# Attention on one Trainium2 core: three PSUM banks for the turned probabilities, one for the values

## The reference, cut to what matters

```python
# selected blocks (all blocks are selected here: 16 of 16), 4 heads of 64, 1024 tokens, blocks of 128 queries
s = jnp.einsum('bqhd,bqkd->bhqk', q, kg) * ATTN_SCALE - slopes[None, :, None, None] * dist[:, None]
p = _masked_softmax(s, ok[:, None])
return jnp.einsum('bhqk,bqkd->bqhd', p.astype(vg.dtype), vg)
...
# sliding window of 512 keys: the same, with 0 <= dist < 512
...
# forgetting attention: s + (fq - fk), keys up to the query, values of its own for each head
```

## Time and profile before

| | us |
|---|---|
| median of three runs | 1512.06 |
| lowest and highest | 1507.91 and 1513.5 |
| the profiled execution, as timed | 1509.91 |
| its span, first to last instruction | 1508.3 |
| TensorE busy with matmuls, of the span | 1368.0 (91%) |
| VectorE, ScalarE, GpSimd busy | 611.7, 516.6, 368.3 |

### The profile page before, as it was taken

How to read it: one execution, slowest core, us unless ns; L and a number is a source line. 1 busy time by engine, 2 the same in 40 slices (tenths; PEclk the granted TensorE clock), 3 DMA queues, 4 the chain that set the end, 5 groups by cost and what they waited for, 6 DMA issues and landing times. The chain is left out here.

```text
span 1508.3 us, 23664 instructions
## 1 busy us (share of the span) xinstructions
PE 1368.0 (91%) x8917; PEld 1185.3 (79%) x8917; DVE 611.7 (41%) x1593; ACT 516.6 (34%) x962; POOL 368.3 (24%) x463
## 2 busy tenths in 40 slices
PE   5999999999999999978888978979985999999965
PEld 3999999999888989956665657968865888888832
DVE  6222212222423324034667557863563233333317
ACT  5422222222122221126545656530001333434336
POOL 5211150020202000002333214621133322322307
PEclk9999999999999999969999999989995999999978
DMA  7244393162624224872004018762117787888954
GB/s 211 71 156 147 122 245 117 58 180 72 188 58 152 78 69 69 186 213 40 1 2 161 16 40 265 233 213 84 63 35 189 237 286 250 265 280 273 326 220 181
DMA packets 188963, 228.29 MB, mean 151 GB/s; under 512 B 47607, under 2 KB 157303, under 8 KB 187487
## 3 DMA queue, kind: packets, MB, share of 16 engines
q1 hardware_dynamic: 176270, 186.25, 41.1%
q0 software_dynamic: 12592, 40.71, 8.7%
HBM read 167.89 MB, written 60.19 MB: 151 GB/s over the span
## 5 line engine op out<-in xcount | busy, mean ns | idle before, releaser
L1255 PE MATMUL psum<-proj_x_hi,proj_w_hi 128*128 128x362 f32 (+1 forms) x1056 | 357.4, 338 | 3.4 <-DVE proj_w_lo L1380 2.2
L1255 PE MATMUL psum<-proj_x_hi,proj_w_lo 128*128 128x362 f32 (+1 forms) x1056 | 346.9, 329 | 0.0
L1255 PE MATMUL psum<-proj_x_lo,proj_w_hi 128*128 128x362 f32 (+1 forms) x1056 | 346.8, 328 | 0.0
L1255 PEld LDWEIGHTS psum<-proj_x_hi,proj_w_hi 128*128 128x128 f32 x1056 | 199.6, 189 | 10.4 <-POOL proj_x_lo L1461 2.5
L1255 PEld LDWEIGHTS psum<-proj_x_lo,proj_w_hi 128*128 128x128 f32 x1056 | 199.9, 189 | 0.0
L1255 PEld LDWEIGHTS psum<-proj_x_hi,proj_w_lo 128*128 128x128 f32 x1056 | 199.3, 189 | 0.0
L1380 DVE TENSOR_TENSOR proj_w_lo<-proj_w_raw,proj_w_hi 128x1024 fp32r<-128x1024 f32 x44 | 54.4, 1237 | 273.8 <-ACT proj_w_hi L1288 273.7
L1317 ACT ACTIVATE proj_sig<-psum,proj_bias 128x362 f32<-128x362 f32 (+1 forms) x72 | 40.4, 564 | 240.6 <-PE psum L1255 228.0
L2809 PEld LDWEIGHTS psum<-moe_xgt,expert_gate_w 128*128 128x128 f32 x512 | 85.2, 194 | 13.2 <-issue 13.2
L2809 PE MATMUL psum<-moe_xgt,expert_gate_w 128*128 128x192 f32 x512 | 92.1, 334 | 0.7 <-ACT moe_xgt L2854 0.7
L2809 PE MATMUL psum<-moe_xgt,expert_up_w 128*128 128x192 f32 x512 | 88.4, 326 | 0.0
(11 more groups left out here) (479 smaller groups left out, 2406.6 us busy)
## 6 DMA issues: line engine op xcount, KB each, us to landing
proj_w_raw<-in_w_in SPq DMA_DIRECT2D x43, 512.0 KB, 5.1
expert_gate_w<-in_moe_w_gate SPq DMA_DIRECT2D x16, 1024.0 KB, 5.6
expert_up_w<-in_moe_w_up SPq DMA_DIRECT2D x16, 1024.0 KB, 11.1
expert_down_w<-in_moe_w_down SPq DMA_DIRECT2D x16, 1024.0 KB, 8.0
merge_sig<-gate_scratch SPq DMA_DIRECT2D x24, 544.0 KB, 4.1
gate_scratch<-proj_sig SPq DMA_DIRECT2D x48, 181.0 KB, 2.0
feature_scratch<-proj_feat SPq DMA_DIRECT2D x13, 512.0 KB, 3.0
token_scratch<-proj_tok SPq DMA_DIRECT2D x10, 512.0 KB, 5.2
```

Of the source, the lines that this page charges most:

```text
L1255: mm = nc.tensor.matmul(k.ps[u % RING][:, 0:w], b[wt][:, x % 2, kk, :], b[xx][:, kk, a0:a0 + w], start=(kk == 0 and i == 0), stop=(kk == K ...
```

## The change

The groups of turned probabilities go round three banks, 4, 5 and 6, so that a group waits for the copy of the group three before it and no more for that two before it. The values of all units are accumulated in bank 7, so that the values of unit u wait for the output of unit u - 1, and no more for that of unit u - 2. Nothing else is touched: the number of instructions and their order are the same on every engine.

```diff
-    bank_of = {x: 4 + n % 2 for n, x in enumerate(groups)}
+    bank_of = {x: 4 + n % 3 for n, x in enumerate(groups)}
...
                     G = groups_upto(u) + g
-                    if G >= 2:
-                        name, count = copied(*groups[G - 2])
+                    if G >= 3:
+                        name, count = copied(*groups[G - 3])
                         pe.wait_ge(s[name], count)
...
                 pe.wait_ge(s["dve_copied"], on_dve)
-                if u >= 2:
-                    pe.wait_ge(s["out_done"], u - 1)
+                if u >= 1:
+                    pe.wait_ge(s["out_done"], u)
                 for j in range(nb):
...
-                        mm = nc.tensor.matmul(k.ps[6 + u % 2][64 * e:64 * e + 64, 0:P], z[:, f + j, c0:c0 + HD], b["probs_t"][:, u % 2, 2 * j + e, :], start=(j == 0), stop=(j == nb - 1))
+                        mm = nc.tensor.matmul(k.ps[7][64 * e:64 * e + 64, 0:P], z[:, f + j, c0:c0 + HD], b["probs_t"][:, u % 2, 2 * j + e, :], start=(j == 0), stop=(j == nb - 1))
...
-                nc.vector.tensor_tensor(dst, k.ps[6 + u % 2][:, 0:P], b["probs_t"][:, u % 2, 2 * blocks(u)[1], :], ALU.mult).then_inc(s["out_done"], 1)
+                nc.vector.tensor_tensor(dst, k.ps[7][:, 0:P], b["probs_t"][:, u % 2, 2 * blocks(u)[1], :], ALU.mult).then_inc(s["out_done"], 1)
```

## The result

| | before | after |
|---|---|---|
| median of 5 runs each, us | 1510.32 | 1496.39 |
| lowest and highest, us | 1505.71 and 1513.5 | 1495.18 and 1500.01 |
| the profiled execution, as timed, us | 1509.91 | 1497.76 |
| its span, us | 1508.3 | 1496.1 |
| ratio after / before, 95% interval | | 0.9941 [0.9918, 0.9964] |

The changed kernel is faster, by 0.6%. Two repetitions further down gave 0.996 and 0.9967, so the first measurement is the largest of three; their mean is 0.9956, 6.6 us.

A forecast was written before the change was run, and what follows sets the result against it. TensorE was taken to set the attention stage's pace, with 9.4 us of waits for copies within reach. Step gains summed to 5.7 us, clock and single values bank to nothing: 1512.06 - 5.7 = 1506.4 us, range 1501.8 to 1511.3.

The forecast's parts named there:

- TensorE's clock: Half-clock stretches in the attention stage, about 1.5 us each; open from -3 to +3 us, taken as nothing.
- Step 2: Attention stage: g2 done early, g3 starts at 688.22, g4 follows at 688.65 instead of waiting until 689.55; gain 0.9 us.
- Step 10: Attention stage: g3 no longer waits 0.84 us for VectorE's copy of g1 and follows g2; gain 1.05 us.
- Step 20: Attention stage: g2's 0.66 us wait for g0's copy goes, since the copy three groups back is long done; gain 0.65 us.
- Steps 32 and 33: Attention stage: g0 goes at once and g4 comes earlier, 0.9 us; then the wait before g4 goes, 0.4 us.
- Steps 36 and 40: Late ScalarE copy of g0: g2 goes ahead but g3 needs that copy; one group's length, 0.4 us, gained at each.
- Step 3: Attention stage: a 0.4 us wait before g4, counted as nothing because GpSimd's ratio is next late in step 4.
- Step 6: Attention stage: taken as one of three instances of the late g0 copy, gaining one group's length, 0.4 us.
- The end: Steps 46 and 47: the turns of unit 47 get their bank one copy sooner; gain 0.6 us.
- rival (b): Attention stage: idling only moves to TensorE's next wait; 1.6 us off, 1510.5 us, chance 0.18.
- rival (a): Attention stage: two half-clock stretches do not occur, 2 x 1.4 us besides 5.7; 8.5 us off, 1503.6 us, chance 0.16.
- Rival (c): Attention stage: closer-packed groups make the clock drop in four more stretches, cancelling the gain; 0 us, 1512 us, chance 0.09.

The follow-up runs named there:

- again_before: The kernel before, run again without an edit; 1509.77 us, one look.
- again_before2: The kernel before, run a third time without an edit; 1510.09 us, one look.
- one_bank: The kernel before with only the values of all units moved to bank 7, groups still in two banks; 1506.43 against 1507.49 us, 0.9983.
- wait_two: The changed kernel's banks, but each group waits for the copy two groups back as before; 1508.3 us against 1507.49 of the kernel before, 1.0005.
- again_after2: The changed kernel, run a third time without an edit; 1503.34 us against 1508.4 of the kernel before, 0.9967.
- fox_two: The changed kernel, but groups of the last sixteen units also wait for the copy two back; 1504.82 us against 1507.49 of the kernel before, 0.9975.
- again_after: The changed kernel, run a second time without an edit; 1501.08 us against 1507.49 of the kernel before, 0.996.
- again_after3: The changed kernel, run a fourth time without an edit; 1501.81 us, one look.
- task_first: The changed kernel with ScalarE's side task, from step 3 on, directly behind the copies, ahead of the exponentials; 1495.83 us against 1508.4 of the kernel before, 0.9919.
- fill: The kernel before with unneeded turns, 14 and 16, added in TensorE's stalls of steps 13 and 36, all waits kept; 1506.42 against 1508.4 us, 0.9982.

## Why the prediction was wrong in size

The forecast had the mechanism of the waits right. It was wrong in the term for TensorE's clock, which it put at nothing.

**The waits.** Predicted 5.7 us, measured 4.9.

- Step 2: 0.9, measured 0.82. Step 10: 1.05, measured 0.95. Step 20: 0.65, measured 0.72. Steps 32 and 33: 0.9 + 0.4, measured 1.34 (that g1 of step 32 starts "0.45 us earlier than now" is 0.1 us too little, and enters no sum). Steps 36 and 40: 0.4 each, measured 0.44 and 0.42. The reasoning "what a wait is worth is not its length" held: 2.39 us of waiting in step 36 yielded 0.44 us.
- Step 3's 0.4 us were counted as nothing because of GpSimd's ratio in step 4. That wait did grow, from 0.45 to 0.91 us, and nothing is left of the gain at step 10.
- Step 6: 0.4, measured 0. I took it as a third instance of step 36 without reading what stands behind it. GpSimd frees the ratio of unit 6 at about 711.7 in after and 711.9 in before, and the unit's last turn needs it. This is the end of the step after:

```profile
711.14 0.44 PE L1697 MATMUL psum<-const,attn_scores 128*128 128x128 f32 x2 [1.15 <-ACT attn_probs_t L1999]
...
711.29 0.40 POOL L1928 TENSOR_TENSOR attn_ratio<-z_gates,attn_inv 128x128 f32<-128x128 f32 x1
...
711.75 0.33 PE L1697 MATMUL psum<-const,attn_ratio 128*128 128x128 f32 x1 [0.17 <-POOL attn_ratio L1928]
```

- The end: 0.6, measured 0.18. I miscounted the groups there. Three back from g0 of unit 47 lies g0 of unit 46, whose copy stands behind ScalarE's exponentials and is still late:

```profile
885.45 0.84 ACT L1999 COPY attn_probs_t<-psum 128x512 f32<-128x512 f32 x2
...
886.16 1.07 PE L1697 MATMUL psum<-const,attn_scores 128*128 128x128 f32 x8 [0.17 <-ACT attn_probs_t L1999]
```

**Does it carry to the end?** Yes. `branch_t`'s wait stayed at 7.7 us, and rival (b), the idling that only moves, is refuted beyond the steps named.

**One bank for the values.** Nothing, as forecast, down to the 0.36 us of values(35), measured as 0.39 in the shadow of the stall.

**TensorE's clock: the step that failed.** The prediction bounded the term at -3 to +3 us and then said "I take nothing, since each end has but a few tenths of idling to turn it". The lower bound was met to 0.2 us: the profile has two falls fewer, 1.6 us each instead of the 1.4 worked out from the earlier trace rows. They were not the two that the prediction had in mind, though. It named those behind steps 6 and 36; the one behind step 6 is still there in after (713.4 to 716.8 us), and the other that went is step 13's, of which it said only that the change "moves everything else against them". The value in between was wrong. Its own numbers spoke otherwise: the fall of the earlier trace rows stood behind a stall of 2.39 us in one piece, and the same text had worked out that g2 moves into the middle of it. That is not a few tenths of idling but a stall cut in two, of which the longer piece is 1.34 us and both together 1.73. In the profiled runs the clock fell at these two places in 11 of 11 cases where the old wait held and nothing filled the stall (5 at step 13, 6 at step 36), and in 3 of 11 where the new one did (1 of 5, 2 of 6). Taken as frequencies, this is four fifths of a fall at the first place and two thirds at the second, about 1.5 x 1.6 = 2.3 us on average: an estimate, from few profiles. With the waits that makes 7.2 us; the four stages of the changed kernel average 207.8 us, the three of before 215.2, 7.4 us apart; the three ratios average to 6.6 us.

By this, rival (a), 8.5 us off with a chance of 0.16, is what the first profile shows in kind, and the average lies between it and the forecast. That the stage of this profile is 8.5 us shorter too is luck: the rival adds 5.7 and 2.8 us, the profile 4.9, 3.2 and 0.4. Rival (c) and the rule cited from the Trainium skill ("TensorE: Matmul & The Clock Gate", section "A second HAM failure mode: psum-queue depth-cycling") pointed the other way. Here a kernel that cycled through banks already had fewer falls at these two places with one bank more; the measurement decides, for this kernel.

**What else separates 1506.4 from 1496.39.** The base, 1512.06, was a median of three; later medians of before are 1510.32, 1507.49, 1508.4 and 1506.82. And the profiled one of the first runs of after had a rest of the program at the short end of its scatter (607.2 of 607.2 to 612.6): of the 12.2 us between the two spans 4.8 lie there. The second measurement, 1501.08, misses the range by under 1 us, the third, 1503.34, lies in it. The effect itself, 0.3 to 0.6%, was forecast as 0.38%.

**Why the clock fell in one profile and not in another.** At step 13 the third bank takes nothing away: the stall is 1.69 us long in all ten profiles that leave it unfilled, the instructions around it are the same, and the nearest wait removed is in step 10, over 10 us earlier. What differs is where the stall lies in time. In each trace the changes of the granted clock, from the first to the last, lie on one regular grid of moments. This is the moment of the grid that lies inside the stall, or the next one behind it, in us:

| kernel | the stall | moment | clock behind it |
|---|---|---|---|
| before | 752.00 to 753.69 | 754.18, behind | fell |
| again_before | 752.51 to 754.20 | 754.20, at its end | fell |
| again_before2 | 754.62 to 756.31 | 756.52, behind | fell |
| one_bank | 758.33 to 760.01 | 760.34, behind | fell |
| wait_two | 750.84 to 752.53 | 753.06, behind | fell |
| again_after2 | 750.92 to 752.61 | 753.85, behind | fell |
| fox_two | 751.33 to 753.01 | 751.39, inside | no |
| after | 750.88 to 752.57 | 750.96, inside | no |
| again_after | 748.83 to 750.51 | 749.31, inside | no |
| again_after3 | 749.58 to 751.26 | 749.73, inside | no |

So the third bank does not shorten this stall; by the waits that it removes ahead of it, it moves the stall against the grid, and the fall comes or not by that. In again_after2 it came although the new wait held. At step 36 the place matters too: of the six profiles with the new wait, the two pieces of the stall lie between the same two moments in the two where the clock fell (again_after, task_first), and in none of the other four. But there the change also takes idling away. With the old wait the clock fell in six of six, and in before a moment lay inside the stall (853.16, in 852.55 to 854.94) and did not spare the fall.

**Open.** This is read from the traces; no run here moves a stall without changing a wait. The share of the clock at step 13, some 1.3 us of the estimate above, is therefore not the third bank's own: any change ahead of that stall could bring it or take it back. At step 36 the shorter idling is a mechanism, and fox_two and fill both bear it out.

## What to carry to other kernels

Price a buffer's extra copy by the next thing that is late: with one bank more, a stall behind a late copy yields only the work that can go ahead of it, and a repeated pattern is read to its end at every instance. Where a stall of the pacing engine is followed by a stretch at the lower clock, add the fall to the price of the stall, by its frequency over several profiles, since one profile can show two falls too many or too few; and count it as the change's own only where the change takes idling away, not where it moves a stall. And put a short copy that frees a PSUM bank ahead of long work on the engine that makes it: on ScalarE this shortened the stage by another 5 us, where the third bank had brought 7.

## What was not expected of the hardware

- A fall of the clock behind a stall of 1.7 to 2.4 us lasts 3.4 us and costs 1.6 us, nearly as much as the stall; it comes in some executions of one kernel and not in others (at step 13 in one of the four profiles of the changed kernel, behind a stall of the same length, at another place in time).
- 14 turns that nobody needs, 1.75 us of them in a stall of about that length, leave the time of the stall as it was and take 1.57 us off what follows.
- The part of the program that no kernel here touches, 610 us long, varies from 607.2 to 612.6 us between profiled executions, and the start of the stage from 679.5 to 687.4 us among the twelve profiles with an unchanged beginning. A difference of two single spans says little below 5 us; the same steps, compared one by one, agree to 0.1 us.
